# A two-block network kernel whose state-space scan handles channel groups one by one, and the same with groups taken in pairs

## The chip, the cores and the metric

One core of a Trainium2 chip runs the whole program. The metric is device time in microseconds (us). The kernel before has a median of 4561.05 us over 3 runs (4560.25 to 4565.51).

## What is computed

Two blocks run over 256 tokens of width 2048. Block one mixes windowed attention with a two-directional complex state-space scan (S5), followed by a product-key retrieval of experts (PEER); block two has a latent attention with a recurrent branch, and PEER again. All arithmetic is float32. The change touches only the scan. It is, for each of 64 groups of 16 channels, 64 complex states and two directions:

```
bu = einsum('bsgc,gnc->bsgn', u, b_bar)
_, states = lax.associative_scan(_ssm_combine, (a, bu), reverse=reverse, axis=1)
y = real(einsum('bsgn,gcn->bsgc', states, c_mat))
```

`_ssm_combine` multiplies the decays and adds the decayed left value. The results of both directions are added, `ssm_d * u` is added, and the sum goes through GELU to a gated linear unit.

## The kernel before

**Tiles and steps.** The 1024 scan channels are 8 tiles of 128 (index `k`, `SSM_K` = 8). A tile has 8 groups of 16 channels; two groups share the 128 partitions (2 x 64 states), which gives 4 pairs of groups (`q`, `PAIRS`) and two directions (`d`): 8 steps `s` a tile, with `q, d = s // 2, s % 2`. The complex recurrence is turned into two real scans: the product B times u is rotated by the phase of the step (multiplied by cosines and sines of the time index), two real scans run along time with a fixed decay, and the result is rotated back. C times the rotated states is then summed over the two directions into the output.

**What each engine does for a step.** GpSimd (POOL, L461) spreads the B matrices of the step into `b_pad`, 128 x 256, zero outside the step's 32 channels. TensorE (PE) transposes its two parts (`b_transposes`, L588), ScalarE (ACT) copies them to `b_t` (L956), and PE multiplies all 128 channels of u by them (`b_times_u`, L598) into the bank `mb[s % 2]`. ACT makes cosines and sines for the step (L961) from the phase that VectorE (DVE) worked out in the step before. DVE reads the bank (L1353, L1354; this counts up `bu_used`), forms the scan's inputs, scans (L1368), waits until the C product of the step before has read its states (`y_done`), rotates back (L1375, L1376) and forms `zr_e` (L1378, L1379; this counts up `de_ready`). PE multiplies by C (`c_times_states`, L610), 128 x 32 weights, into partitions 32q to 32q+31 of the bank `tb[1]`.

**Start and end of a tile.** PE transposes the tile's C matrices (L624), DVE masks and scales them (L1325 to L1344). After the eighth step DVE adds `ssm_d * u` (L1383). The tile's B and C matrices (`b_st`, `c_st`) are loaded by eight DMAs of ACT's queue (`load_bc`, L918 and L921). `reload_bc(k)` issues them for the next tile behind everything that ACT does in tile `k`, once the pads and C transposes of `k` are done.

**Dense work in between.** PE alone has other work in the scan: the projections that block one needs later. A *dense slot* (`dense_slot`, L531) is 8 matmuls of 128 x 512, each of which the profile shows as two passes, so 16. Eight slots fill the banks of group 0 (slots 0 to 3) and group 1 (slots 4 to 7). Tiles 0 to 5 have 8 slots each; tiles 6 and 7 have 4 each. ACT empties group 0 behind the sine of step 3 and group 1 behind the sine of step 7 (`dense_evac`, L947), in tiles 6 and 7 one group behind the sine of step 7.

**What sets the order.** Each engine's order is written out by hand, with semaphores between the engines. PE's order in a tile of 8 slots is: slot 0, C transposes, then the pads of steps 0 and 1 and the product of step 0, then for each step the B product of the next step, the transposes of the one after, one dense slot, and the C product of this step:

```
                for s in range(8):
                    if s < 7:
                        b_times_u(k, s + 1)
                    if s < 6:
                        b_transposes(k, s + 2)
                    if s + 1 in dense:
                        dense_slot(dense[s + 1], r, hT, r * 2)
                    c_times_states(k, s)
```

Weights of the dense slots come through a ring of 8 buffers of 1 MB, refilled by the SP queue.

Of the kernel before, what the change touches and what calls it, by code (L numbers as in the profile page):

```python
# [14 lines left out]
ds = bass.ds  # L15
# [73 lines left out]
def two_blocks(nc, a, out):  # L89

    ctx = ExitStack()
    with ctx:
# [26 lines left out]
        iota_t = cn[:, 128:384]  # L119
        mask_b = cn[:, 384:416].rearrange("p (q b) -> p q b", q=PAIRS)  # L120
        mask_c = cn[:, 416:544]
# [133 lines left out]
        (rA, rB, rZI, rZ, rD, rE, rF, rR, rBP, rBT, rCT, rCP, rPR) = cut(  # L255
            0, [512] * 8 + [512, 512, 512, 512, 256])
        two = lambda r: sc[:, r[0]:r[1]].rearrange("p (c n) -> p c n", c=2)
        bre_e, bim_e, z_in, z_out, zr_e, zi_e, phase, whole = map(two, (rA, rB, rZI, rZ, rD, rE, rF, rR))
        b_pad = sc[:, rBP[0]:rBP[1]].rearrange("p (i a b c) -> p i a b c", i=2, a=2, b=8)
        b_t = sc[:, rBT[0]:rBT[1]].rearrange("p (i a n) -> p i a n", i=2, a=2)  # L260
        c_t = sc[:, rCT[0]:rCT[1]].rearrange("p (d a n) -> p d a n", d=2, a=2)
# [168 lines left out]
        def _(pool):  # L430
# [10 lines left out]
            for half in range(2):  # L441
                rows = slice(64 * half, 64 * half + 64)
                for q in range(PAIRS):
                    st.link(pool.memset(mask_b[rows, q, 2 * q + half:2 * q + half + 1], 1.0))
                of_half = mask_c[rows, :].rearrange("p (q f c) -> p q f c", q=PAIRS, f=2)[:, :, half, :]
                st.link(pool.memset(of_half, 1.0))
# [7 lines left out]
            with pool.Fori(0, SSM_K) as k:  # L454

                pool.wait_ge(bc_loaded, k * BC + BC)
                for s in range(8):
                    q, d = s // 2, s % 2

                    pool.wait_ge(bt_done, k * 8 + s + 1)  # L460
                    pool.tensor_tensor(  # L461
                        b_pad[:, s % 2], b_st[:, :, d, q, :].unsqueeze(2).broadcast_to([P, 2, 8, 16]),
                        mask_b[:, q, :].unsqueeze(1).unsqueeze(3).broadcast_to([P, 2, 8, 16]),
                        ALU.mult).then_inc(bpad_ready, 1)

# [52 lines left out]
        def _(pe):  # L518
# [49 lines left out]

            pe.sem_inc(bt_done, 2)
            pe.sem_inc(bu_done, 2)  # L570
# [11 lines left out]

            def b_transposes(k, s):
                pe.wait_ge(bpad_ready, k * 8 + s + 1)

                pe.wait_ge(bt_evac, k * 8 + s + 2)
                for part in range(2):
                    tr = pe.transpose(tb[0][:, part * P:(part + 1) * P],  # L588
                                      b_pad[:, s % 2, part].rearrange("p b c -> p (b c)"), ident)
                tr.then_inc(bt_done, 1)  # L590

            def b_times_u(k, s):
                pe.wait_ge(bt_evac, k * 8 + s + 3)
                if s == 0:
                    pe.wait_ge(ct_evac, k + 1)
                pe.wait_ge(bu_used, k * 8 + s + 1)
                for part in range(2):
                    mm = pe.matmul(mb[s % 2][:, part * T:(part + 1) * T], b_t[:, s % 2, part, :],  # L598
                                   uT[:, ds(k, 1), :].rearrange("p a n -> p (a n)"), start=(part == 0), stop=True,
                                   skip_group_check=True)  # L600
                mm.then_inc(bu_done, 1)

            def c_times_states(k, s):
                q, d = s // 2, s % 2
                if s == 0:
                    pe.wait_ge(y_evac, k + 1)
                pe.wait_ge(de_ready, k * 8 + s + 3)

                for n, (j, rhs) in enumerate(((0, zr_e[:, 1, :]), (1, zr_e[:, 0, :]))):
                    mm = pe.matmul(tb[1][32 * q:32 * q + 32, 0:T], c_p[:, j, d, q, :], rhs,  # L610
                                   start=(d == 0 and n == 0), stop=(d == 1 and n == 1), skip_group_check=True)
                mm.then_inc(y_done, 1)

            def ssm_tile(k, r, slots):

                every = SLOTS // len(slots)
                dense = {n * every: b for n, b in enumerate(slots)}

                dense_slot(dense[0], r, hT, r * 2)
                pe.wait_ge(bc_loaded, k * BC + BC)  # L620

                pe.wait_ge(bu_used, k * 8 + 1)
# [4 lines left out]
                b_transposes(k, 0)  # L627
                b_times_u(k, 0)
                b_transposes(k, 1)
                for s in range(8):  # L630
                    if s < 7:
                        b_times_u(k, s + 1)
                    if s < 6:
                        b_transposes(k, s + 2)
                    if s + 1 in dense:
                        dense_slot(dense[s + 1], r, hT, r * 2)
                    c_times_states(k, s)


            pe.wait_ge(sp_done, 2)  # L640
            with pe.Fori(0, SSM_K - 2) as k:
                ssm_tile(k, k + R_QKV, range(SLOTS))
# [230 lines left out]
        def _(act):  # L873
# [23 lines left out]

            act.sem_inc(bt_evac, 2)
            norm_rms(0)
# [50 lines left out]
            def ssm_tile(k, i, groups):  # L950

                for s in range(8):

                    act.wait_ge(bt_done, k * 8 + s + 3)
                    act.wait_ge(bu_done, k * 8 + s + 1)
                    act.activation(b_t[:, s % 2].rearrange("p a n -> p (a n)"),  # L956
                                   tb[0][:, 0:2 * P], ACT.Copy).then_inc(bt_evac, 1)

# [6 lines left out]
            def reload_bc(k):  # L965

                act.wait_ge(bpad_ready, k * 8 + 8)
                act.wait_ge(ct_done, k + 1)
                load_bc(k + 1)
# [259 lines left out]
        def _(v):  # L1229
# [76 lines left out]
            def phase_1(k, s):  # L1306

                q, d = s // 2, s % 2
                return v.scalar_tensor_tensor(
# [9 lines left out]
            def ssm_tile(k):  # L1319
# [19 lines left out]

                v.wait_ge(y_done, k * 8 + 1)  # L1340
                st.wait()
# [3 lines left out]
                for s in range(8):  # L1345
                    q, d = s // 2, s % 2
                    both = lambda t: t.unsqueeze(1).broadcast_to([P, 2, T])
# [24 lines left out]

                    v.wait_ge(y_done, k * 8 + s + 1)
                    st.wait(z3)
# [5 lines left out]

                v.wait_ge(y_done, k * 8 + 9)
                kk = ds(k, 1)
# [457 lines left out]
```

## Time and profile before

| | us |
|---|---|
| median of 3 runs | 4561.05 |
| runs | 4560.25, 4561.05, 4565.51 |
| span of the profiled execution | 4559.0 |
| PE busy / DVE busy / ACT busy / POOL busy in it | 1629.2 / 3389.3 / 397.1 / 2108.9 |
| scan, from its first dense slot to the last tile's output | 83.2 to 692.2 |

The shares of the whole span say little of the scan: two long stretches of it are the expert retrievals, in which DVE and the gathers of POOL are busy and PE is not. The scan is one stretch of 609 us and is read by itself. A weight load (PEld) lies beside a running matmul. The own time of the profiled execution is not listed apart from its span; the span is 1.2 us under the lowest of the three runs.

### The profile page before, as it was taken

What the parts mean: (1) busy time and instruction counts of PE and PEld (TensorE: products, weight loads), DVE (VectorE), ACT (ScalarE), POOL (GpSimd) and SP (SyncE); (2) the same over time, 40 slices, a digit from 0 to 9 for tenths busy, and PEclk for the clock granted to TensorE, in tenths of its full rate; (3) what the DMA queues carried; (4) which work ended last, traced back from release to release, by engine and by line L of the source; (5) the groups of instructions that cost most, each with busy time, mean ns of one, the idle gap of its engine ahead of it and who ended that gap; (6) DMA issues with size and microseconds to landing.
All of it is one profiled execution on the core that took longest, in us unless ns stands there. A gap on an engine that the chain in (4) does not pass through costs nothing. (4 is left out here: it accounts for less than half of the span.)

```text
span 4559.0 us, 21846 instructions
## 1 busy us (share of the span) xinstructions
PE 1629.2 (36%) x5521; PEld 961.5 (21%) x5521; DVE 3389.3 (74%) x4309; ACT 397.1 (9%) x780; POOL 2108.9 (46%) x1162
## 2 busy tenths in 40 slices
PE   8999978998900000000000099888000000000000
PEld 6444434444800000000000066457000000000000
DVE  3777795301099999999999913411999999999999
ACT  1111114300100000000000013301000000000000
POOL 0000000000076777776777700000777767767767
PEclk9999989999955555555555599799555555555555
DMA  6343422344399999999999953132999999999999
GB/s 201 111 110 112 117 67 85 103 142 144 126 411 397 379 398 400 378 396 394 388 394 400 374 159 132 56 129 76 405 387 394 400 382 394 408 384 390 398 389 377
DMA packets 283029, 1286.59 MB, mean 282 GB/s; under 512 B 46993, under 2 KB 56033, under 8 KB 150881
## 3 DMA queue, kind: packets, MB, share of 16 engines
q0 software_dynamic: 147456, 1073.81, 57.7%
q1 hardware_dynamic: 100400, 200.81, 13.6%
q10 hardware_dynamic: 35120, 11.33, 1.0%
q8 instruction: 26, 0.43, 0.0%
q14 instruction: 27, 0.21, 0.0%
HBM read 1283.77 MB, written 2.10 MB: 282 GB/s over the span
## 5 line engine op out<-in xcount | busy, mean ns | idle before, releaser
L1578 DVE SCALAR_TENSOR_TENSOR xs<-big,sc,xs 128x2048 f32<-128x2048 f32 x512 | 1203.7, 2351 | 51.0 <-DVE sc L1568 2.1
L1560 DVE CUSTOM_DVE_ANT_0 big<-big,hs 128x2048 f32<-128x2048 f32 x512 | 1137.8, 2286 | 34.8 <-remote 10.3
L488 POOL DMA_INDIRECT big<-in_peer_down,sc x256 | 518.2, 2024 | 638.0 <-issue 635.4
L531 PE MATMUL bank<-wring,ht 128*128 128x512 f32 (+1 forms) x1792 | 778.5, 592 | 3.3 <-ACT ht L888 1.7
L488 POOL DMA_INDIRECT big<-in_peer_u,sc x256 | 518.2, 2024 | 405.0 <-DVE sc L1547 320.4
L488 POOL DMA_INDIRECT big<-in_peer_up,sc x256 | 506.0, 1977 | 247.6 <-DVE xs L1578 172.2
L488 POOL DMA_INDIRECT big<-in_peer_v,sc x256 | 506.1, 1977 | 246.6 <-DVE xs L1578 171.1
L772 PE MATMUL bank<-cn,sc 80*128 80x80 f32 x1 | 0.4, 393 | 1381.4 <-DMA sc<-in_rec_out_norm_g 1381.4
L531 PEld LDWEIGHTS bank<-wring,ht 128*128 128x128 f32 x1792 | 339.7, 192 | 402.1 <-issue 395.9
L545 PE MATMUL bank<-ht,wring 128*128 128x256 f32 x1792 | 387.9, 379 | 2.6 <-ACT ht L888 2.6
L545 PEld LDWEIGHTS bank<-ht,wring 128*128 128x128 f32 x1792 | 340.2, 190 | 49.6 <-issue 2.4
L461 POOL TENSOR_TENSOR sc<-big,cn 128x256 f32<-128x256 f32 x64 | 50.5, 795 | 605.4 <-DMA big<-in_ssm_c_im 319.4
L772 PEld LDWEIGHTS bank<-cn,sc 80*128 80x128 f32 x1 | 0.2, 180 | 1381.6 <-DMA sc<-in_rec_out_norm_g 1381.6
L1073 ACT ACTIVATE sc<-sc 128x16 f32<-128x16 f32 x32 | 6.9, 215 | 2436.0 <-DVE sc L1560 2436.0
L1512 DVE COPY sc<-ht 128x256 f32 (+1 forms) x32 | 9.2, 287 | 242.5 <-ACT ht L1062 242.5
L657 PE MATMUL bank<-wring,hs 128*128 128x512 f32 x256 | 117.9, 601 | 5.2 <-ACT hs L984 5.2
L507 POOL MEMSET big<- 128x384 f32 x1 | 0.4, 418 | 235.4 <-DVE big L1750 235.4
L1375 DVE TENSOR_TENSOR sc<-sc,big 128x512 f32<-128x512 f32 x64 | 43.9, 687 | 77.7 <-PE bank L610 77.5
L1499 DVE TENSOR_TENSOR xs<-bank,xs 128x512 f32 x8 | 5.2, 685 | 113.1 <-PE bank L531 113.1
L610 PE MATMUL bank<-sc 128*32 128x256 f32 x256 | 72.6, 409 | 46.3 <-DVE sc L1379 46.3
L1368 DVE TENSOR_TENSOR_SCAN sc<-sc 128x256 f32<-128x256 f32 x128 | 84.1, 697 | 1.3 <-DVE sc L1314 0.2
L1481 DVE TENSOR_TENSOR big<-bank,big 128x512 f32 x8 | 5.2, 685 | 101.0 <-PE bank L531 101.0
(308 smaller groups left out, 2055.2 us busy)
## 6 DMA issues: line engine op xcount, KB each, us to landing
wring<-in_w_in SPq DMA_DIRECT2D x84, 1024.0 KB, 5.3
wring<-in_w_out SPq DMA_DIRECT2D x32, 1024.0 KB, 5.0
wring<-in_w_attn_o SPq DMA_DIRECT2D x16, 1024.0 KB, 5.1
wring<-in_peer_w_query SPq DMA_DIRECT2D x16, 1024.0 KB, 5.0
wring<-in_peer_w_q SPq DMA_DIRECT2D x16, 1024.0 KB, 5.0
wring<-in_glu_w_a SPq DMA_DIRECT2D x8, 1024.0 KB, 5.0
wring<-in_glu_w_b SPq DMA_DIRECT2D x8, 1024.0 KB, 5.0
big<-in_peer_down,sc POOLq DMA_INDIRECT x256, 9.5
```

The costliest lines, as they stand in the source:

```text
L461: pool.tensor_tensor(b_pad[:, s % 2], b_st[:, :, d, q, :].unsqueeze(2).broadcast_to([P, 2, 8, 16]), mask_b[:, q, :].unsqueeze(1).unsqueeze ...
L488: pool.indirect_dma_start(out=gslot[:, slot, :], out_offset=None, in_=table[0], in_offset=bass.IndirectOffsetOnAxis(ap=usub(rST)[:, b * TO ...
L531: mm = pe.matmul(dense_bank[2 * pair + t][:, 0:w_cols], lhs[:, k, t * P:(t + 1) * P], wslot[:, b, kk * w_cols:(kk + 1) * w_cols], start=(k ...
L545: mm = pe.matmul(dense_bank[2 * g + c // 2][:, (c % 2) * T:(c % 2 + 1) * T], wslot[:, b, kk * 512 + c * P:kk * 512 + (c + 1) * P], rhs[:, ...
L610: mm = pe.matmul(tb[1][32 * q:32 * q + 32, 0:T], c_p[:, j, d, q, :], rhs, start=(d == 0 and n == 0), stop=(d == 1 and n == 1), skip_group_ ...
L657: mm = pe.matmul(dense_bank[2 * pair + t][:, :], yT[:, k, t * P:(t + 1) * P], wslot[:, b, kk * 512:(kk + 1) * 512], start=(k == 0), stop=( ...
L1073: act.activation(sub(rGE)[:, b * TOPK:(b + 1) * TOPK], sub(rAC)[:, b * TOPK:(b + 1) * TOPK], ACT.Gelu).then_inc(gelu_ready, 1)
L1368: z3 = st.add(v.tensor_tensor_scan(zo, radius, zi, 0.0, ALU.mult, ALU.add))
L1375: st.add(v.tensor_tensor(zr_e, both(z_out[:, 0, :]), e, ALU.mult))
L1512: st.link(v.tensor_copy(w1, kscore[:, ds((unit - base) * 256, 256)]))
L1560: v.tensor_tensor_reduce(gslot[:, slot, :], gslot[:, slot, :], h[:, t, :], 1.0, 0.0, ALU.mult, ALU.add, sub(rAC)[:, b * TOPK + kk:b * TOPK ...
L1578: v.scalar_tensor_tensor(x[:, t, :], gslot[:, slot, :], wt[:, kk:kk + 1], x[:, t, :], ALU.mult, ALU.add).then_inc(gused[slot], 1)
```

## The change

Steps are taken in pairs `m` = 0 to 3, steps 2m and 2m+1: `q_and_d` gives both the same direction and neighbouring pairs of groups (q = 0, 1, then 0, 1 backwards, then 2, 3, and 2, 3 backwards).

- `b_pad` holds the whole tile: POOL makes it in four operations of half the size, PE turns it in four transposes into one bank, ACT copies it with one copy of 128 x 512.
- `b_times_u(k, m)` multiplies only the 32 channels of a step (rows 32q to 32q+31 of the array); the two steps of a pair alternate, one bank each. `c_times_states(k, m)` alternates the pair's two column strips.
- There are two buffers for the rotated states; `y_done` counts pairs, and a step waits only for the pair before its own.
- PE's order is new. The C and B transposes come first, then slot 0, then the B product of pair 0. In pair m of a tile with 8 slots come two dense slots with the B product of pair m+1 ahead of the second, then the C product. Pair 0 has only slot 1 left, with the B product of pair 1 ahead of it. The loop over tiles 0 to 5 is written out.

```
+            def b_times_u(k, m):
+
+                pe.wait_ge(bu_used, k * 8 + 2 * m + 2)
                 for part in range(2):
+                    for s in (2 * m, 2 * m + 1):
+                        q, d = q_and_d(s)
+                        rows = slice(32 * q, 32 * q + 32)
+                        mm = pe.matmul(mb[s % 2][:, part * T:(part + 1) * T], b_t[rows, d, part, :],
+                                       uT[rows, k, :], start=(part == 0),
+                                       stop=True, skip_group_check=True)
+                        if part == 1:
+                            mm.then_inc(bu_done, 1)
+
+            def c_times_states(k, m):
+                if m == 0:
                     pe.wait_ge(y_evac, k + 1)
+                pe.wait_ge(de_ready, k * 8 + 2 * m + 4)
+
+                for n in range(2):
+                    for s in (2 * m, 2 * m + 1):
+                        q, d = q_and_d(s)
+                        mm = pe.matmul(tb[1][32 * q:32 * q + 32, 0:T], c_p[:, n, d, q, :], states[s % 2][:, 1 - n, :],
+                                       start=(d == 0 and n == 0), stop=(d == 1 and n == 1), skip_group_check=True)
                 mm.then_inc(y_done, 1)
 
             def ssm_tile(k, r, slots):
 
-                every = SLOTS // len(slots)
-                dense = {n * every: b for n, b in enumerate(slots)}
-
-                dense_slot(dense[0], r, hT, r * 2)
+                per = len(slots) // 4
                 pe.wait_ge(bc_loaded, k * BC + BC)
...
+                pe.wait_ge(bpad_ready, k * 4 + 4)
+                pe.wait_ge(bt_evac, k + 1)
+                for d in range(2):
+                    for part in range(2):
+                        j = d * 2 + part
+                        tr = pe.transpose(tb[0][:, j * P:(j + 1) * P],
+                                          b_pad[:, d, part].rearrange("p q f c -> p (q f c)"), ident)
+                tr.then_inc(bt_done, 1)
+                dense_slot(slots[0], r, hT, r * 2)
+                pe.wait_ge(bt_evac, k + 2)
+                pe.wait_ge(ct_evac, k + 1)
                 b_times_u(k, 0)
...
+                for m in range(4):
+                    for b in slots[max(1, m * per):m * per + per]:
+                        if b == slots[m * per + per - 1] and m < 3:
+                            b_times_u(k, m + 1)
+                        dense_slot(b, r, hT, r * 2)
+                    if m < 3 and not slots[max(1, m * per):m * per + per]:
+                        b_times_u(k, m + 1)
+                    c_times_states(k, m)
...
             def ssm_tile(k, i, groups):
 
+                act.wait_ge(bt_done, k + 2)
+                act.wait_ge(bu_done, k * 8 + 2)
+                act.activation(b_t.rearrange("p d a n -> p (d a n)"), tb[0][:, :], ACT.Copy).then_inc(bt_evac, 1)
                 for s in range(8):
...
-                    v.wait_ge(y_done, k * 8 + s + 1)
+                    v.wait_ge(y_done, k * 4 + s // 2 + 1)
```

ACT's order for the rest of a tile is as before: sines 0 to 3, the emptying of group 0, sines 4 to 7, the emptying of group 1, the eight load DMAs.

**First place: PE at the start of a tile of 8 slots.** The names are those of the banks and buffers; `L531` is a dense slot, `L624` and `L588` are the C and B transposes, `L598` a B product, `L610` a C product. Before:

```order
L531 MATMUL bank<-wring,ht 128x512 [waits wfull0]
L531 MATMUL bank<-wring,ht 128x512 x7
...
L622 ISA [waits bc_loaded]
L624 MATMUL bank<-cn,big 128x128 [waits bu_used]
L624 MATMUL bank<-cn,big 128x128 x3
...
L588 MATMUL bank<-cn,sc 128x128 [waits bt_evacuated]
...
L598 MATMUL bank<-hs,sc 128x256 x2
...
L598 MATMUL bank<-hs,sc 128x256 [waits bu_used,bt_evacuated]
...
L531 MATMUL bank<-wring,ht 128x512 [waits wfull1]
...
L610 MATMUL bank<-sc 32x256 [waits states_ready,y_evacuated]
```

Now (`L615` C transposes, `L623` B transposes, `L590` B product, `L604` C product):

```order
L615 MATMUL bank<-cn,big 128x128 [waits bu_used,bc_loaded]
L615 MATMUL bank<-cn,big 128x128 x3
L623 MATMUL bank<-cn,sc 128x128 [waits bt_evacuated,bpad_ready]
L623 MATMUL bank<-cn,sc 128x128 x3
L531 MATMUL bank<-wring,ht 128x512 [waits wfull0,pair_evac0]
L531 MATMUL bank<-wring,ht 128x512 x7
L590 MATMUL bank<-hs,sc 128x256 [waits bu_used,ct_evacuated,bt_evacuated]
L590 MATMUL bank<-hs,sc 128x256 x3
L590 MATMUL bank<-hs,sc 128x256 [waits bu_used]
L590 MATMUL bank<-hs,sc 128x256 x3
L531 MATMUL bank<-wring,ht 128x512 [waits wfull1]
...
L604 MATMUL bank<-sc 32x256 [waits states_ready,y_evacuated]
```

The wait for the loaded matrices now stands ahead of slot 0, and two B products stand in a row with no slot between them.

**Second place: PE from slot 2 to slot 4, in the changed kernel.** Slot 3 is the last of group 0:

```order
L531 MATMUL bank<-wring,ht 128x512 [waits wfull2]
...
L590 MATMUL bank<-hs,sc 128x256 [waits bu_used]
...
L531 MATMUL bank<-wring,ht 128x512 [waits wfull3]
...
L604 MATMUL bank<-sc 32x256 [waits states_ready]
...
L531 MATMUL bank<-wring,ht 128x512 [waits wfull4,pair_evac1]
```

Slot 3 was in step 2, ahead of the C product of step 2; it is now in pair 1, behind the B product of steps 4 and 5.

**Third place: ACT in the middle of a tile, in the changed kernel** (`L959` is a sine, `L947` the emptying of a dense bank, `wused3` the end of slot 3, `wused7` of slot 7):

```order
L959 ACTIVATE big<-sc 128x512 [waits states_ready,phase_ready]
L947 ISA [waits wused3]
L947 ACTIVATE big<-bank 128x512
L947 ISA
L947 ACTIVATE big<-bank 128x512
L957 REGISTER_ALU
L959 ACTIVATE big<-sc 128x512 [waits states_ready,phase_ready]
```

The sine of step 4 stands behind the emptying that waits for slot 3, as before; what moved is slot 3 on PE.

## Rows read from the trace of the kernel before

**Rows 1.** Busy time by stretch: start:end, length, engines, granted clock, DMA share, GB/s.
```profile
170.00:248.00 78.00, 73.88 (x213) 34.55 (x212) 58.23 (x112) 9.73 (x20) 5.97 (x8) 1.00 0.40 113
248.00:562.00 314.00, 297.39 (x849) 138.70 (x848) 232.95 (x448) 38.91 (x80) 24.70 (x32) 0.99 0.39 112
562.00:631.00 69.00, 51.40 (x148) 24.90 (x147) 59.15 (x112) 8.42 (x18) 6.78 (x8) 0.88 0.21 67
```
**Rows 2.** Who waited for whom, scan only: us in total, times, longest us.
```profile
DVE sc L1375 <- PE bank L610: 77.5, 33, 3.4
```
**Rows 3.** Timeline, one step on PE: start us, us, engine, line, operation, count.
```profile
190.78 1.05 PE L610 MATMUL bank<-sc 128*32 128x256 f32 x4
191.76 1.13 PE L598 MATMUL bank<-hs,sc 128*128 x4
192.72 0.38 PE L588 MATMUL bank<-cn,sc 128*128 128x128 f32 x2
192.94 7.03 PE L531 MATMUL bank<-wring,ht 128*128 128x512 f32 x16
199.90 1.05 PE L610 MATMUL bank<-sc 128*32 128x256 f32 x4
```
**Rows 4.** Timeline, one step on DVE, and the start of the next.
```profile
94.52 0.69 DVE L1353 TENSOR_TENSOR sc<-bank,big 128x512 f32<-128x512 f32 x1 [0.19 <-DVE sc L1344]
95.12 0.68 DVE L1354 TENSOR_TENSOR sc<-bank,big 128x512 f32<-128x512 f32 x1
99.15 0.68 DVE L1375 TENSOR_TENSOR sc<-sc,big 128x512 f32<-128x512 f32 x1
...
101.15 0.68 DVE L1353 TENSOR_TENSOR sc<-bank,big 128x512 f32<-128x512 f32 x1
```
**Rows 5.** Timeline, end of tile 1 and start of tile 2, PE.
```profile
236.94 1.05 PE L610 MATMUL bank<-sc 128*32 128x256 f32 x4
...
241.15 7.13 PE L531 MATMUL bank<-wring,ht 128*128 128x512 f32 x16
248.12 0.60 PE L624 MATMUL bank<-cn,big 128*128 128x128 f32 x4
```
**Rows 6.** The same place, ACT's queue: the first of the loads.
```profile
237.49 0.38 ACTq L918 DMA_DIRECT2D big<-in_ssm_b_re  x1
```
**Rows 7.** The same place and an earlier one, POOL: the pads.
```profile
170.97 0.62 POOL L461 TENSOR_TENSOR sc<-big,cn 128x256 f32<-128x256 f32 x1 [3.69 <-PE bank L588]
...
246.29 1.20 POOL L461 TENSOR_TENSOR sc<-big,cn 128x256 f32<-128x256 f32 x2 [42.62 <-DMA big<-in_ssm_c_im]
```
**Rows 8.** Busy time by stretch around an idle time of PE (columns as in 1).
```profile
567.00:573.00 6.00, 0.00 (x0) 0.00 (x0) 5.97 (x14) 0.90 (x2) 0.35 (x1) 0.82 0.00 0
573.20:575.00 1.80, 1.80 (x4) 0.50 (x4) 1.80 (x4) 0.00 (x0) 0.00 (x0) 0.50 0.00 0
575.00:576.80 1.80, 1.80 (x5) 1.41 (x5) 1.80 (x5) 0.00 (x0) 0.00 (x0) 0.50 0.00 0
577.30:584.30 7.00, 7.00 (x18) 3.01 (x16) 6.97 (x14) 0.90 (x2) 1.77 (x1) 0.98 0.00 0
```
**Rows 9.** Timeline, ACT behind step 3: bank emptied, sine of step 4, DVE of step 3.
```profile
200.21 1.08 ACT L947 ACTIVATE big<-bank 128x512 f32 x2 [6.74 <-PE bank L531]
200.99 0.69 DVE L1375 TENSOR_TENSOR sc<-sc,big 128x512 f32<-128x512 f32 x1 [1.26 <-PE bank L610]
...
201.44 0.64 ACT L961 ACTIVATE big<-sc 128x512 f32<-128x512 f32 x1
```
**Rows 10.** Timeline, the scan's first PE work; DVE's first bank read in tiles 6 and 7, last operation of step 7.
```profile
83.16 7.13 PE L531 MATMUL bank<-wring,ht 128*128 128x512 f32 x16 [0.80 <-DVE sc L1296]
...
566.34 0.69 DVE L1353 TENSOR_TENSOR sc<-bank,big 128x512 f32<-128x512 f32 x1 [0.20 <-DVE sc L1344]
...
635.82 0.69 DVE L1353 TENSOR_TENSOR sc<-bank,big 128x512 f32<-128x512 f32 x1 [0.20 <-DVE sc L1344]
...
689.03 0.42 DVE L1379 TENSOR_TENSOR sc<-sc 128x256 f32<-128x256 f32 x1
```

More of the change, by code:

```diff
@@ L253, in cut @@
             return res
-        (rA, rB, rZI, rZ, rD, rE, rF, rR, rBP, rBT, rCT, rCP, rPR) = cut(
-            0, [512] * 8 + [512, 512, 512, 512, 256])
+        (rA, rB, rZI, rZ, rD, rD2, rE, rF, rR, rBP, rBT, rCT, rCP, rPR) = cut(
+            0, [512] * 9 + [512, 512, 512, 512, 256])
         two = lambda r: sc[:, r[0]:r[1]].rearrange("p (c n) -> p c n", c=2)
-        bre_e, bim_e, z_in, z_out, zr_e, zi_e, phase, whole = map(two, (rA, rB, rZI, rZ, rD, rE, rF, rR))
-        b_pad = sc[:, rBP[0]:rBP[1]].rearrange("p (i a b c) -> p i a b c", i=2, a=2, b=8)
-        b_t = sc[:, rBT[0]:rBT[1]].rearrange("p (i a n) -> p i a n", i=2, a=2)
+        bre_e, bim_e, z_in, z_out, zi_e, phase, whole = map(two, (rA, rB, rZI, rZ, rE, rF, rR))
+        states = (two(rD), two(rD2))
+        b_pad = sc[:, rBP[0]:rBP[1]].rearrange("p (d a q f c) -> p d a q f c", d=2, a=2, q=PAIRS, f=2)
+        b_t = sc[:, rBT[0]:rBT[1]].rearrange("p (d a n) -> p d a n", d=2, a=2)
+        q_and_d = lambda s: (s // 4 * 2 + s % 2, s // 2 % 2)
         c_t = sc[:, rCT[0]:rCT[1]].rearrange("p (d a n) -> p d a n", d=2, a=2)
@@ L442, in _ @@
                 rows = slice(64 * half, 64 * half + 64)
-                for q in range(PAIRS):
-                    st.link(pool.memset(mask_b[rows, q, 2 * q + half:2 * q + half + 1], 1.0))
+                st.link(pool.memset(mask_b[rows, half:half + 1], 1.0))
                 of_half = mask_c[rows, :].rearrange("p (q f c) -> p q f c", q=PAIRS, f=2)[:, :, half, :]
@@ L456, in _ @@
                 pool.wait_ge(bc_loaded, k * BC + BC)
[L457 to L464, printed above, removed]
+                pool.wait_ge(bt_done, k + 1)
+                for d in range(2):
+                    for part in range(2):
+                        pool.tensor_tensor(
+                            b_pad[:, d, part], b_st[:, part, d].unsqueeze(2).broadcast_to([P, PAIRS, 2, 16]),
+                            mask_b.unsqueeze(1).unsqueeze(3).broadcast_to([P, PAIRS, 2, 16]),
+                            ALU.mult).then_inc(bpad_ready, 1)
             pool.wait_ge(y_evac, SSM_K + 1)
@@ L592, in b_times_u @@
[L592 to L601, printed above, removed]
@@ L603, in c_times_states @@
-            def c_times_states(k, s):
-                q, d = s // 2, s % 2
-                if s == 0:
-                    pe.wait_ge(y_evac, k + 1)
[L607 to L611, printed above, removed]
+                    for s in (2 * m, 2 * m + 1):
[6 more added lines that the diff above has]
+                            mm.then_inc(bu_done, 1)
@@ L626, in ssm_tile @@
                 tr.then_inc(ct_done, 1)
-                b_transposes(k, 0)
-                b_times_u(k, 0)
[L629 to L637, printed above, removed]
+                pe.wait_ge(bpad_ready, k * 4 + 4)
+                pe.wait_ge(bt_evac, k + 1)
+                for d in range(2):
+                    for part in range(2):
+                        j = d * 2 + part
[5 more added lines that the diff above has]
+                pe.wait_ge(ct_evac, k + 1)
+                b_times_u(k, 0)
+                for m in range(4):
[6 more added lines that the diff above has]
+                    c_times_states(k, m)
             pe.wait_ge(sp_done, 2)
-            with pe.Fori(0, SSM_K - 2) as k:
+            for k in range(SSM_K - 2):
                 ssm_tile(k, k + R_QKV, range(SLOTS))
@@ L1345, in ssm_tile @@
                 for s in range(8):
-                    q, d = s // 2, s % 2
+                    q, d = q_and_d(s)
+                    zr_e = states[s % 2]
                     both = lambda t: t.unsqueeze(1).broadcast_to([P, 2, T])
```

26 lines of the change are left out of this document (8 added, 18 removed).

## The prediction, made before the changed kernel had run

> **What bounds the kernel now.** The page gives shares over 4559 us, but the change touches one stretch of 609 us, so I first cut the trace there by busy time. In tiles 1 to 5 PE is busy 371 of 392 us and DVE 291 [rows 1]: PE bounds the tiles with eight dense slots. In tile 6, with four slots, DVE is busy 59 of 69 us and PE 51: there DVE's chain of steps bounds. The list of waits agrees: DVE stood 77.5 us before L1375 until PE had made a C product that was queued behind a dense slot [rows 2]. The timeline then gives the prices. A PE step is 9.12 us from C product to C product: 0.98 for the C product, 0.96 for the B product, 0.22 for two transposes, 6.96 for the slot [rows 3]. A DVE step that does not wait is 6.6 us (94.52 to 101.15); it has read the bank 1.3 us after its start, and reaches the state buffer at 4.6 [rows 4]. A tile with eight slots takes on average (566.34 - 94.52) / 6 = 78.6 us from first bank read to first bank read [rows 4, 10].
>
> **What it removes.** Per tile, 12 of 16 transposes: 12 x 0.11 = 1.3 us of PE. The B and C products go from 16 of 0.96 to 0.98 us to 8 pairs. No row shows two strips of the array together, so a pair is bounded: 0.98 if two strips cost as one, 1.84 if they run one behind the other (8 passes of 0.215 and one change-over of 0.12, from [rows 3]). I take 1.3, just under the middle: each strip's two passes must follow each other, but the other strip's can lie beside the second. That frees 8 x 1.94 - 8 x 1.3 = 5.1 us, together some 6.5 us of PE a tile. The Trainium skill, "TensorE: Matmul & The Clock Gate", Part 3 (Packing small matmuls), says that matmuls on different strips start about 4 ns apart and a pack takes the time of one matmul; no row here shows it, and by it the pair would be 0.98 and the whole change 53 us slower instead of 68. The waits of DVE at L1375 shrink too. POOL's pads halve in size and in number. DVE has the same instructions as before. This is work; what counts is the order.
>
> **What it moves, first place: the load is uncovered.** Slot 7 ends at 236.94. ACT then issues eight loads, the first at 237.49, and POOL can start at 246.29: 9.35 us [rows 5 to 7]; the other tile boundaries of the trace are up to 0.7 shorter, and I take 9.0. Before, the C product of step 7 and slot 0 of the next tile lay in it, and PE met the loaded matrices only at 248.12. Now the C and B transposes wait for the load ahead of slot 0, and slot 7 lies ahead of the last C product. So PE has one C product (1.3) to do in 9.0 us, then waits for the pads: four operations of half the size of one that took 0.62, so 0.3 to 0.6 each, 1.8 in all. Queued behind it on PE is everything, slot 0 included.
>
> **Second place: pair 0 has no cover.** The B product of pair 1 needs both banks read, which is one DVE step and 1.3 us after DVE's start: 6.6 + 1.3 = 7.9. No slot lies between it and the B product of pair 0.
>
> **Third place: slot 3 holds back a sine.** ACT makes the sine of step 4 only after emptying group 0. From slot 3's end (199.9) to the end of that sine (202.1) it is 2.1 us [rows 3, 9]. Slot 3 now comes after the B product of pair 2, when DVE has already finished step 3; DVE waits for it.
>
> **The clock.** After 6 us without matmuls the granted clock is 0.50, the 1.2 GHz level, for the next two products, 3.6 us of work, and 0.98, the 2.4 GHz level, after that [rows 8]: a loss of 1.8 us. Both new idle times are longer, so I charge 1.8 twice a tile, bounds 0 and 3.6 each (none lost, or twice as long).
>
> **The walk through a tile of eight slots**, from the moment the load has landed, with 6.9 for a slot (its 6.96 less a change-over that is in the products):
> - transposes with their wait for the pads 2.4; slot 0 6.9; clock 1.8: 11.1. B product of pair 0 to DVE's first read 1.4 (four passes of C to L1375 take 1.1 [rows 3, 9], and 0.3 for the pair): DVE starts at **12.5**.
> - plus 7.9: 20.4. B product 1.3, slot 1 6.9, clock 1.8, C product 1.3: 31.7. DVE has finished step 1 at 25.7, so PE is the later.
> - slot 2 6.9, B product 1.3, slot 3 6.9: 46.8. Sine 2.1: DVE starts step 4 at 48.9 (it had been free since about 41).
> - plus 7.9: 56.8; PE had slot 4 done by 55. B product 1.3, slot 5 6.9, C product 1.3, slots 6 and 7 13.8: **80.1**. Load 9.0: **89.1**.
>
> That is 10.5 more than 78.6, the sum of 16 to 17 us of new idle time of PE and of lost clock, less the work freed. DVE reads the first bank of tile 0 at 83.2 [rows 10] + 0.9 + 6.9 + 1.4 = 92.4 instead of 94.5, as the matrices of tile 0 are there long before. So tile 6 starts at 92.4 + 6 x 89.1 = 627.0 instead of 566.3 [rows 10]: **+60.7**.
>
> **Tiles 6 and 7, four slots.** The B product of pair 1 goes at 7.9 after DVE's start, of pair 2 at 13.3 + 7.9 = 21.2; then slot 1, clock and C product end at 32.5. DVE waits 1.2 there for the buffer, and about as long a pair later. The B product of pair 3 goes at 35.7; with slot 2, clock, C product and slot 3 it is 53.9. Load 9.0 and start 12.5: 75.4, against 69.5 before (635.82 - 566.34 [rows 10]): **+5.9**. In tile 7 DVE needs 8 x 6.63 + 2.4 = 55.4 for its eight steps, before 689.45 - 635.82 = 53.6 [rows 10]: **+1.8**. The written-out PE loop costs nothing that a row could show: tiles 6 and 7 were written out before, and a slot there takes 7.0 us too [rows 8]. DVE, ACT and the weight ring have slack where PE idles.
>
> **The sum**: 60.7 + 5.9 + 1.8 = 68.4 us. All that follows the scan waits for its output, so the end moves by as much. The profiled span of 4559.0 becomes 4627.4; it stands 2.05 under the median, which becomes 4561.05 + 68.4 = 4629.5, rounded **4630**.
>
> **Rivals.**
> - *Two strips cost as one* (a pair 0.98). Six pairs lie on the walk: 6 x 0.32, 0.3 less of slow clock, 2.2 a tile, 13 us, and 2 in the last tiles: 4615. For it: the strips are separate parts of the array, and a pair's outputs lie in separate banks or partitions. Against: each product is two passes that reuse one strip. The page named above makes this rule.
> - *Strips run one behind the other*, so that this part of the change does nothing (a pair 1.84): 6 x 0.54 and 0.5 of clock, 3.7 a tile, 22 us, and 3: 4655.
> - *The clock does not fall, or work between the idle times restores it*: less 1.8 x 2 x 6 and 5 in the last tiles, 27 us: 4603. Against it are rows 8.
> - *The load is covered, and the tiles get shorter: faster.* If the new matrices were there when the last C product ends, and slot 3 were done in time for the sine, the walk would be 0.9 + 6.9 + 1.4 + 7.9 + 9.5 + 16.4 + 16.4 + 15.1 = 74.5: 4.1 a tile under 78.6, 25 us, and some 5 in the last: about 4531. That is what 6.5 us less of PE work promises. It decides in favour if the load lands within 1.3 us of slot 7's end instead of 9.0, and ACT's order speaks against it: the loads are still last.
>
> **Chances.** Forecast 0.48; strips as one 0.18; strips one behind the other 0.18; clock 0.07; load covered 0.05; the rest 0.04, longer idle times and more slow clock than charged. A measurement of this kernel tells 0.2%, 9 us, from no change. All but the covered load are over that: slower 0.93, same 0.02, faster 0.05. The range runs from the clock case to strips in sequence with a load of 9.4 and some clock more: 4602 to 4665.
>
> **What would show it.** Right: tiles of 89 us from first bank read to first bank read; PE idle 7 to 8 us behind the last C product of a tile, released by the load; 8 us between the first two B products, released by DVE's L1354; DVE idle 7 to 8 us before step 4, released by ACT's sine; granted clock 0.5 at the start of slots 0 and 1; a pair at 1.2 to 1.4 us. Wrong: transposes right behind the last C product, tiles under 78 us, or a DVE that never waits at step 4.

## The result, and the profile after

The changed kernel takes **4629.49 us** (median of 4 runs, 4626.96 to 4632.71), beside 4561.3 for the kernel before (4 runs, 4560.25 to 4565.51). The ratio is 1.0148, with a 95% interval of 1.0134 to 1.0163: slower by 68.2 us, where 68.4 were forecast. The profiled execution has a span of 4628.2 us and a mean granted clock of 0.670 (before 4559.0 and 0.683). All four engines are busy for less time than before, PE for 26 us less (1603.1), and the kernel takes longer.

Busy time by stretch of the changed kernel; the columns are those of [rows 1], the five busy times those of PE, PEld, DVE, ACT and POOL. The stretches are tile 0, tile 1, tiles 2 to 5 and tile 6:

```profile
83.00:170.00 87.00, 69.01 (x201) 30.37 (x202) 59.16 (x116) 8.38 (x15) 0.02 (x1) 0.92 0.38 114
170.00:259.00 89.00, 71.10 (x201) 31.30 (x201) 56.96 (x112) 7.58 (x13) 1.45 (x4) 0.88 0.33 99
259.00:613.00 354.00, 284.08 (x800) 125.40 (x800) 227.85 (x448) 30.33 (x52) 5.88 (x16) 0.89 0.33 100
613.00:688.00 75.00, 47.03 (x136) 20.88 (x136) 56.96 (x112) 6.61 (x11) 1.47 (x4) 0.75 0.21 62
```

A tile of eight slots has 71 of 89 us of PE in it, before 74 of 78 [rows 1]. PE no longer bounds these tiles, nor does DVE with 57 of 89: 18 us of each tile are PE standing still, before 4. The granted clock, 1.00 before, is 0.88.

To measure a tile I take DVE's first scan in it (L1367, and L1368 of the kernel before). The differences from tile to tile are 89.6, 89.0, 88.6, 88.8, 88.7, 88.6 and, from tile 6 to tile 7, 75.0. Before they were 79.9, 78.1, 79.7, 78.1, 78.0, 78.0 and 69.5.

The list of waits in the scan (us in total, times, longest us):

```profile
PE bank L590 <- DVE sc L1353: 93.8, 18, 8.1
PE bank L615 <- DMA big<-in_ssm_c_im: 49.9, 7, 7.7
DVE sc L1352 <- PE bank L590: 60.0, 8, 8.3
DVE sc L1352 <- ACT big L959: 49.6, 6, 8.3
...
DVE sc L1374 <- PE bank L604: 19.4, 10, 2.6
```

The first four are new. The first is for the most part the B product of pair 1 with no cover (the uncovered pair): eight of its 18 waits are 8.1 us long. The second is the load that nothing covers. The third is DVE waiting for the first B product of a tile, which now stands behind slot 0: 8.11 us in tile 1, while slot 0 runs from 172.42 to 181.02. This wait hangs on the load too; with the load out of the way (e1) it falls from 60.0 to 21.6 us in total. The fourth is the sine behind slot 3. DVE's waits for C products, 77.5 us before [rows 2], are the last row, 19.4: the change does what it says there.

The timeline of PE over tile 1 (start us, us, engine, line, operation, count, and in brackets the idle time ahead and what ended it), to hold against [rows 3, 5]:

```profile
161.17 1.06 PE L604 MATMUL bank<-sc 128*32 128x256 f32 x8
169.88 1.11 PE L615 MATMUL bank<-cn,big 128*128 128x128 f32 x4 [7.65 <-DMA big<-in_ssm_c_im]
171.51 1.12 PE L623 MATMUL bank<-cn,sc 128*128 128x128 f32 x4 [0.52 <-POOL sc L461]
172.42 8.68 PE L531 MATMUL bank<-wring,ht 128*128 128x512 f32 x16
181.02 1.13 PE L590 MATMUL bank<-hs,sc 32*128 32x256 f32 x8
190.26 2.08 PE L590 MATMUL bank<-hs,sc 32*128 32x256 f32 x8 [8.10 <-DVE sc L1353]
192.26 9.07 PE L531 MATMUL bank<-wring,ht 128*128 128x512 f32 x16
201.26 1.06 PE L604 MATMUL bank<-sc 128*32 128x256 f32 x8
202.25 7.13 PE L531 MATMUL bank<-wring,ht 128*128 128x512 f32 x16
209.31 1.13 PE L590 MATMUL bank<-hs,sc 32*128 32x256 f32 x8
210.38 7.13 PE L531 MATMUL bank<-wring,ht 128*128 128x512 f32 x16
217.44 1.06 PE L604 MATMUL bank<-sc 128*32 128x256 f32 x8
...
227.33 1.13 PE L590 MATMUL bank<-hs,sc 32*128 32x256 f32 x8 [1.77 <-DVE sc L1353]
...
250.38 1.06 PE L604 MATMUL bank<-sc 128*32 128x256 f32 x8
258.95 1.12 PE L615 MATMUL bank<-cn,big 128*128 128x128 f32 x4 [7.52 <-DMA big<-in_ssm_c_im]
```

Three idle times, as the walk had them: behind the last C product of a tile, before the B product of pair 1, and a short one before the B product of pair 3. A pair of B products takes 210.38 - 209.31 = 1.07 us and a pair of C products 202.25 - 201.26 = 0.99: a pair on two strips costs what one product cost before (0.98 for C), or 0.11 us more (0.96 for B [rows 3]). Slot 0 takes 8.60 us (172.42 to 181.02) and slot 1 takes 9.00 (192.26 to 201.26); all others of the tile take 6.97 to 7.06.

The granted clock behind the second idle time; the first stretch is the B product of pair 1, the others lie in slot 1 (columns as above):

```profile
189.90:192.10 2.20, 1.84 (x8) 1.18 (x8) 2.20 (x6) 0.00 (x0) 0.00 (x0) 0.50 0.00 0
192.30:194.30 2.00, 2.00 (x5) 0.97 (x4) 2.00 (x5) 0.63 (x1) 0.00 (x0) 0.50 0.00 0
194.30:196.30 2.00, 2.00 (x4) 0.84 (x3) 1.97 (x5) 0.00 (x0) 0.00 (x0) 0.53 0.00 0
196.30:198.30 2.00, 2.00 (x6) 0.89 (x5) 2.00 (x5) 0.00 (x0) 0.00 (x0) 1.00 0.00 0
```

PE is at 0.50, the 1.2 GHz level, from 190.3 to about 196.3. That is 6 us of work after 8 us of nothing, not the 3.6 us that the kernel before showed [rows 8].

The middle of the tile, ACT and DVE (rows between them left out):

```profile
217.65 1.08 ACT L947 ACTIVATE big<-bank 128x512 f32 x2 [16.73 <-PE bank L531]
...
218.62 0.63 ACT L959 ACTIVATE big<-sc 128x512 f32<-128x512 f32 x1
...
219.36 0.69 DVE L1352 TENSOR_TENSOR sc<-bank,big 128x512 f32<-128x512 f32 x1 [8.27 <-ACT big L959]
```

ACT waits for slot 3, which ends at 217.44, empties group 0, and only then makes the sine of step 4. DVE has been idle for 8.27 us. From slot 3's end to DVE's read it is 1.92 us (forecast 2.1).

Most of the load's time is its issue. Of the 8.7 us from the end of slot 7 (161.17) to the first transposes (169.88), ACT's queue spends 6.2 on issuing the eight DMAs, the first at 161.82 and the last done at 167.98; one of them alone shows 2.02 us. From there to the transposes it is 1.9 us.

### The profile page after: what moved, and what is told of

It is laid out like the page before. It is cut to its first block and busy times, and to the rows that moved or that the text cites. A ratio compares the mean times of both kernels' runs of the same rounds, so it can differ in the third digit from the quotient of the medians.

```text
span 4628.2 us, 21289 instructions
## 1 busy us (share of the span) xinstructions
PE 1603.1 (35%) x5425; PEld 936.2 (20%) x5425; DVE 3378.1 (73%) x4309; ACT 381.1 (8%) x724; POOL 2071.0 (45%) x1124
## 5 line engine op out<-in xcount | busy, mean ns | idle before, releaser
L531 PE MATMUL bank<-wring,ht 128*128 128x512 f32 (+1 forms) x1792 | 805.9, 609 | 2.4 <-ACT ht L888 1.7
L531 PEld LDWEIGHTS bank<-wring,ht 128*128 128x128 f32 x1792 | 349.6, 198 | 433.4 <-issue 427.6
L461 POOL TENSOR_TENSOR sc<-big,cn 128x128 f32<-128x128 f32 x32 | 11.9, 402 | 674.7 <-DMA big<-in_ssm_c_im 674.7
L1352 DVE TENSOR_TENSOR sc<-bank,big 128x512 f32<-128x512 f32 x64 | 43.9, 686 | 109.7 <-PE bank L590 60.0
L1367 DVE TENSOR_TENSOR_SCAN sc<-sc 128x256 f32<-128x256 f32 x128 | 81.3, 678 | 1.1
L590 PE MATMUL bank<-hs,sc 32*128 32x256 f32 x256 | 45.7, 484 | 93.8 <-DVE sc L1353 93.8
```

The source lines that it names most:

```text
L461: pool.tensor_tensor(b_pad[:, d, part], b_st[:, part, d].unsqueeze(2).broadcast_to([P, PAIRS, 2, 16]), mask_b.unsqueeze(1).unsqueeze(3).br ...
L531: mm = pe.matmul(dense_bank[2 * pair + t][:, 0:w_cols], lhs[:, k, t * P:(t + 1) * P], wslot[:, b, kk * w_cols:(kk + 1) * w_cols], start=(k ...
L590: mm = pe.matmul(mb[s % 2][:, part * T:(part + 1) * T], b_t[rows, d, part, :], uT[rows, k, :], start=(part == 0), stop=True, skip_group_ch ...
L1352: st.add(v.tensor_tensor(bre_e, both(mb[s % 2][:, 0:T]), e, ALU.mult))
L1367: z3 = st.add(v.tensor_tensor_scan(zo, radius, zi, 0.0, ALU.mult, ALU.add))
```

## The experiments

Eight kernels. The first four ask where the 68 us come from and whether the parts add up; e5 and e6 ask what the strips of the array are worth; e7 and e8 test the clock and the load by themselves. The first four share one set of runs of the kernel before (median 4561.56), the others a second (4562.64), so that a comparison across the two sets carries 1.1 us.

### e1: the load early

```
 # ACT, ssm_tile
+                    if s == 1 and reload:
+                        reload_bc(k)
 ...
-                reload_bc(k)
```

> The changed kernel with one edit: ACT issues the eight loads of the next tile's matrices behind the sine of step 1 instead of behind the emptying of group 1; they only need the pads and C transposes of the tile, which are done at its start. Theory (the uncovered load costs its whole wait): PE's 7.5 us of idle time, 0.5 us for the pads and about 2.5 us of slow clock vanish at six tile ends and some 8 us at the seventh: 71 us less than the changed kernel, about 4558. Rival (DVE's work at the tile's end bounds there, the load only hides it): less than 15 us are gained and the wait before the C transposes goes to DVE.

**4555.95 us**, ratio 0.9988 (0.9978 to 0.9998), 73.5 under the changed kernel, where 71 were expected. Tiles of 77.5 to 78.5 us, 66.1 from tile 6 to tile 7. The timeline of PE in e1 at the same tile boundary:

```profile
159.09 1.06 PE L604 MATMUL bank<-sc 128*32 128x256 f32 x8
160.08 0.66 PE L615 MATMUL bank<-cn,big 128*128 128x128 f32 x4
...
161.01 7.03 PE L531 MATMUL bank<-wring,ht 128*128 128x512 f32 x16
167.97 1.13 PE L590 MATMUL bank<-hs,sc 32*128 32x256 f32 x8
177.20 2.08 PE L590 MATMUL bank<-hs,sc 32*128 32x256 f32 x8 [8.09 <-DVE sc L1353]
```

The transposes stand right behind the last C product, take half as long, and slot 0 takes 6.96 (161.01 to 167.97) instead of 8.60. Moving eight DMA issues gives back more than the whole loss; the other two idle times stay. From the start of the last C product to the B product of pair 0 it is 8.9 us (159.09 to 167.97) instead of 19.85 (161.17 to 181.02). Of these 11.0, 8.2 are idle time of PE (7.65 for the load and 0.52 for the pads), 1.6 the slow clock in slot 0 and about 1 the slow clock in the eight transposes. Where the load is issued is thus the largest part of the damage.

### e2: the sine of step 4 before group 0 is emptied

```
-                ssm_tile(k, k, {3: 0, 7: 1})
+                ssm_tile(k, k, {5: 0, 7: 1})
```

> The changed kernel with one edit: ACT empties group 0 behind the sine of step 5 instead of step 3. Theory (PE bounds the middle of the tile, DVE's idle time there costs only what PE then waits for at the B product of pair 3): DVE's 8.3 us of idle time before step 4 vanish, PE's 1.8 us before the third B product too, 6 x 1.8 = 11 us less than the changed kernel, about 4618. Rival (DVE's idle time counts in full): about 48 us less, 4581.

**4609.62 us**, ratio 1.0106 (1.0089 to 1.0123): 19.9 less than the changed kernel. Tiles of 86.9, 86.5, 85.5, 85.3, 85.5 and 85.4. That is 2.4 to 3.5 a tile, not 1.8 as forecast and not the 8 of the rival: DVE's 8.27 us of idle time were nearly all hidden behind PE. The 1.77 us before the B product of pair 3 are gone. The remainder, 0.6 to 1.7 us a tile, is in most tiles a slightly shorter idle time at the load (6.91 to 7.54 us, in the changed kernel 7.08 to 7.65) and, in tiles 2 to 5, less slow clock: in tile 4 the rows of slots 0 and 1 show 7.81 and 8.64 us, in the changed kernel 8.59 and 9.03. Slots 0 and 1 of tile 1 show none of this (9.05 and 9.27). Why the slow stretches are shorter there, no row tells.

### e3: a slot between the first two B products

```
-                dense_slot(slots[0], r, hT, r * 2)
                 pe.wait_ge(bt_evac, k + 2)
                 pe.wait_ge(ct_evac, k + 1)
                 b_times_u(k, 0)
+                dense_slot(slots[0], r, hT, r * 2)
 ...
+                    if m == 0:
+                        b_times_u(k, 1)
                     c_times_states(k, m)
```

The B product of pair 0 goes ahead of slot 0, and that of pair 1 behind slot 1.

> The changed kernel with one edit in PE's order: the B product of pair 0 stands ahead of slot 0, and slots 0 and 1 stand between it and the B product of pair 1. Theory (8.1 us of PE idle time and 3 us of slow clock between the first two B products are the cost): D7 moves from 80 to 70 us of a tile, 10.5 x 6, and DVE starts 7 us earlier in tiles 6 and 7: 77 us less than the changed kernel, about 4552. Rival (what pair 0 waits for now is found elsewhere, at the load): under 30 us less.

**4570.95 us**, ratio 1.0022 (1.0012 to 1.0031): 58.5 less, where 77 were expected (D7 in the expectation is the end of slot 7, 80.1 in the walk). The idle time of 8.1 us is gone, but a tile takes 80.0 to 82.1 us instead of the 78.6 that this makes. PE in e3, from the end of tile 0 to the start of tile 1:

```profile
131.51 1.13 PE L590 MATMUL bank<-hs,sc 32*128 32x256 f32 x8 [1.76 <-DVE sc L1353]
...
142.32 14.00 PE L531 MATMUL bank<-wring,ht 128*128 128x512 f32 x32
...
168.17 2.08 PE L590 MATMUL bank<-hs,sc 32*128 32x256 f32 x8 [0.77 <-ACT sc L954]
170.17 16.09 PE L531 MATMUL bank<-wring,ht 128*128 128x512 f32 x32
186.20 1.13 PE L590 MATMUL bank<-hs,sc 32*128 32x256 f32 x8
```

and busy time and clock behind the first of these rows:

```profile
132.60:134.60 2.00, 2.00 (x6) 0.94 (x5) 2.00 (x5) 0.00 (x0) 0.00 (x0) 0.71 0.88 335
134.60:136.60 2.00, 2.00 (x4) 0.87 (x3) 1.97 (x5) 0.63 (x1) 0.00 (x0) 0.50 0.00 1
```

Behind the load, which e3 leaves uncovered, PE is as slow as before: slots 0 and 1 take 16.03 us (170.17 to 186.20) where two slots take 13.93 at the upper level (142.32 to 156.25), and the B product of pair 0 takes 2.00. PE also waits 0.77 us ahead of it for ACT's copy of the transposed B matrices, which slot 0 used to cover. And a second slow stretch now comes behind an idle time of 1.76 us (tile 0, slot from 132.57 on, and so in five of the six tiles, not in tile 4), which before the same product of the changed kernel (1.77 us) had cost nothing. The expectation had taken the slow clock away with the idle time; part of it only moved.

### e4: all three at once

ACT as in e1, group 0 emptied behind the sine of step 4 (`{4: 0, 7: 1}`), and on PE, from slot 0 on:

```
+                if per == 2:
+                    plan = "S B0 S B1 S C0 S B2 S C1 S B3 S C2 S C3"
+                else:
+                    plan = "B0 S B1 S C0 B2 S C1 B3 S C2 C3"
```

where `S` is the next dense slot and a number is a pair. The eighth slot lies between C2 and C3, so that every product of a tile of eight slots has a slot ahead of it.

> All three waits taken away: loads behind the sine of step 1, group 0 emptied behind the sine of step 4, and PE's order in a tile of eight slots S B0 S B1 S C0 S B2 S C1 S B3 S C2 S C3 (S a slot, B and C the products of the numbered pair), in tiles 6 and 7 B0 S B1 S C0 B2 S C1 B3 S C2 C3. Theory (pairing frees 7 us of PE a tile, and only the order hid it): a tile takes 67 to 69 us against 88.8 in the changed kernel and 78.6 before, 140 us less than the changed kernel, about 4490, and 70 less than before. Rival (pairing itself costs time, by strips or by the clock): no better than before, 4561.

**4490.82 us** (4487.5 to 4495.65), ratio 0.9847 (0.9831 to 0.9864). This beats both kernels, and the expected time is met. Busy time by stretch of e4, tile 0 and then tiles 1 to 5:

```profile
83.00:150.00 67.00, 65.24 (x199) 28.29 (x197) 56.73 (x111) 7.69 (x13) 1.92 (x4) 1.00 0.43 134
150.00:485.00 335.00, 326.94 (x994) 143.22 (x992) 284.84 (x558) 37.39 (x63) 9.78 (x20) 1.00 0.43 131
```

Tiles 0 to 4 take 67.4 us, tile 5 takes 65.1. PE is busy 327 of 335 us, the clock is 1.00, and a tile has two idle times of PE left: 1.03 us before the B product of pair 1 and 0.73 before the last C product. The three repairs alone gave 73.5, 19.9 and 58.5, in sum 152; together they gave 138.7. They overlap: the 1 us a tile that e2 saves at the load and in slow slots can't be saved again where e1 has covered the load. The plan is not exactly their union either: its order of slots and products is a different one from e3's.

### e5: the strips not alternated

```
-                for part in range(2):
-                    for s in (2 * m, 2 * m + 1):
+                for s in (2 * m, 2 * m + 1):
+                    for part in range(2):
```

and the same in the C product: all passes of one step, then all of the other, on e4.

> The kernel of e4_all_three, with the two steps of a pair no longer alternating: both products of one strip, then both of the other. Theory (passes start in order and a pass waits for its own strip, so strips overlap only where neighbours differ): a pair takes about 1.6 us instead of 1.0, eight pairs a tile in six tiles, about 30 us more than e4_all_three, near 4520. Rival (the engine looks ahead and starts a later pass on a free strip): no change, 4491.

**4490.19 us**, ratio 0.9843 (0.9827 to 0.986): no change from e4. The first 0.2 us of one pair of B products, of these instructions alone (length, busy time of PE and of PEld, clock, DMA share, GB/s; x counts the passes that run in the stretch); e4:

```profile
115.83:116.03 0.20, 0.20 (x2) 0.20 (x4) 1.00 0.00 0
```

and e5:

```profile
115.86:116.06 0.20, 0.20 (x2) 0.20 (x4) 1.00 0.00 0
```

Two passes run at once in either. Written as all of step 2m and then all of step 2m+1, they still start in twos, 13 ns apart instead of 7. The alternating loop of the change is not needed; which part of the chip or of the compilation lets the second step's passes start beside the first's, no row tells.

### e6: both steps of a pair on one strip

```
-                        q, d = q_and_d(s)
+                        q, d = q_and_d(2 * m)
```

in both products, on e4.

> The kernel of e4_all_three, with both steps of a pair sent to the strip of its first step (rows in the B product, output partitions in the C product); the second step's B and C products are therefore computed from the first one's channels and added into its output. Theory (two strips cost as one, and that is what pairing gains): a pair takes 1.85 us instead of 1.0, 0.86 x 8 x 6 = 41 us more than e4_all_three, near 4532. Rival (the pair is short for another reason, such as 32 rows or columns being faster in themselves): a pair stays near 1.0 and the time at 4491.

**4552.16 us** (4545.28 to 4557.26), ratio 0.9977 (0.9967 to 0.9987), 61.3 over e4. PE in e6 at the start of tile 0:

```profile
91.17 1.99 PE L590 MATMUL bank<-hs,sc 32*128 32x256 f32 x8
93.09 7.13 PE L531 MATMUL bank<-wring,ht 128*128 128x512 f32 x16
100.83 1.99 PE L590 MATMUL bank<-hs,sc 32*128 32x256 f32 x8 [0.61 <-DVE sc L1360]
102.75 8.83 PE L531 MATMUL bank<-wring,ht 128*128 128x512 f32 x16
111.51 1.91 PE L604 MATMUL bank<-sc 128*32 128x256 f32 x8
```

and the first 0.2 us of the second of these products, as for e5:

```profile
100.83:101.03 0.20, 0.20 (x1) 0.20 (x2) 1.00 0.65 147
```

One pass at a time, and a pair takes 1.92 us (91.17 to 93.09) or 1.84 (C, 111.51 to 113.35). The upper bound of the prediction was 1.84; the two strips give 0.85 us a pair, 6.9 a tile, of which 0.4 comes back as shorter idle time (0.61 us instead of 1.03). Tile 2, of 73.9 us, is 6.5 longer than in e4. Tiles 0, 1, 3 and 4, of 75.5, have a slow clock on top: slot 2 takes 8.76 us (102.75 to 111.51) after an idle time of only 0.61. The expected 41 us left that out, and tiles 6 and 7: from tile 6 to tile 7 it is 75.9 us instead of 65.5, and tile 7 is 8.3 longer from its first scan to its last. A pair of B products there, behind idle times of 3.1 and 3.4 us, takes 3.2 to 3.7 us (537.40 to 541.08, 583.93 to 587.17).

### e7: idle time filled with work that nobody needs

```
                 b_times_u(k, 0)
+                if per == 2:
+                    for n in range(8):
+                        pe.matmul(tb[0][:, :], ident, hT[:, 2 * n:2 * n + 2, :].rearrange("p k n -> p (k n)"),
+                                  start=True, stop=True)
```

The changed kernel with a slot's worth of matmuls in the uncovered pair.

> The changed kernel with 8 extra matmuls of 128 x 512 (16 passes, 6.9 us) behind the B product of pair 0 in tiles 0 to 5, into the bank that held the transposed B matrices, where PE otherwise idles 8.1 us. Nothing reads them. Theory (the idle time costs a second time, by the clock: the B product of pair 1 and slot 1 take 11.1 us instead of 8.1): granted clock 1.0 there, 3.0 us less a tile, 18 us less than the changed kernel, about 4611. Rival (those two are slow for another reason, such as reads that collide with DVE's): no change, 4629.

**4612.19 us**, ratio 1.011 (1.0093 to 1.0127): 17.3 less than the changed kernel, with more work. PE of e7 around that place:

```profile
186.10 1.13 PE L590 MATMUL bank<-hs,sc 32*128 32x256 f32 x8 [1.03 <-DVE sc L1357]
187.16 7.13 PE L531 MATMUL bank<-wring,ht 128*128 128x512 f32 x16
```

The granted clock is 1.00 in every stretch from 181 to 199. So the clock's share of the uncovered pair is 17.3 us over six tiles, 2.9 a tile: 0.94 in the B product (2.00 instead of 1.06) and 1.94 in slot 1 (9.00 instead of 7.06). The waiting itself, 8.1 us a tile, is the larger share and is untouched. The tiles do not show this evenly: five of the six are 3.1 to 3.9 us shorter than in the changed kernel, and tile 2 only 0.8, because its slot 5 runs slow behind an idle time of 1.77 us (307.00 to 315.76, 8.76 us).

### e8: slot 0 behind the transposes, in the kernel before

```
-                dense_slot(dense[0], r, hT, r * 2)
                 pe.wait_ge(bc_loaded, k * BC + BC)
 ...
                 b_transposes(k, 0)
+                dense_slot(dense[0], r, hT, r * 2)
                 b_times_u(k, 0)
```

> The kernel before with one edit: slot 0 moved behind the C transposes and the first B transposes, so that the load is uncovered and nothing is paired. Theory (the order ahead of slot 0, not the pairing, exposes the load): PE idles about 5 us at each of six tile ends, plus 0.6 for the pads and 1.8 of slow clock, less small waits that vanish, 6 to 7 us a tile, 38 us more than before, about 4600. Rival (the load is late only because the changed kernel ends its tiles sooner): under 10 us more, 4570.

**4594.77 us**, ratio 1.0075 (1.0059 to 1.0092): 32 slower than the kernel before. PE of e8 at the start of tile 1:

```profile
164.34 1.11 PE L623 MATMUL bank<-cn,big 128*128 128x128 f32 x4 [4.09 <-DMA big<-in_ssm_c_im]
165.25 0.63 PE L588 MATMUL bank<-cn,sc 128*128 128x128 f32 x2
165.68 8.95 PE L531 MATMUL bank<-wring,ht 128*128 128x512 f32 x16
```

This one move, with nothing of pairs or strips, makes the load's idle time and the slow clock behind it (slot 0 takes 8.79 us) and lengthens tiles to 83.1 to 85.0 us. The idle time is 4.1 to 4.9 us instead of 7.6, because in the old order slot 7 ends two C products before the tile does, and PE waits 2.2 us between them for DVE while the load is under way. The six tiles cost 33 us; ahead of them and in tile 6 the edit saves some (DVE's first bank read comes 3.4 us earlier, and from tile 6 to tile 7 it is 65.9 us instead of 69.5), which the expected 38 had left out.

## Why the prediction was right, and where it was not

**The walk.** The forecast was 89.1 us a tile and 75.4 from tile 6 to tile 7; the chip took 88.6 to 89.6, and 75.0. The same points in tile 1, from the start of its transposes (169.88):

| | forecast | measured |
|---|---|---|
| DVE's first read | 12.5 | 12.4 (182.28) |
| B product of pair 1 | 20.4 | 20.4 (190.26) |
| C product of pair 0 done | 31.7 | 32.4 (202.25) |
| DVE starts step 4 | 48.9 | 49.5 (219.36) |
| B product of pair 3 | 56.8 | 57.5 (227.33) |
| slot 7 done | 80.1 | 80.5 (250.38) |
| transposes of the next tile | 89.1 | 89.1 (258.95) |

All three new idle times are where the walk had them, released by what it named: the load, DVE's second bank read, ACT's sine. The step on which everything hung, "the load is uncovered", was tested from both sides: e1 takes it back and gains 73.5 us, e8 puts it into the kernel before and loses 32. The second, "pair 0 has no cover", holds as well: its idle time is the 8.1 us of the waits, and e3 and e7 get 58.5 and 17.3 us back there. The third, "slot 3 holds back a sine", has its 8.27 us of idle DVE, but e2 shows that little of it reached the end: 19.9 us over the tiles, of about 50.

**Two terms were mis-sized and cancelled.** "I take 1.3, just under the middle" for a pair of strips: it is 1.07 for B and 0.99 for C. The rival *two strips cost as one* was the truth of that term, and the reason against it, that each product is two passes that reuse one strip, does not hold: the other strip's passes lie wholly beside them. That made the walk about 1.5 us a tile too long. The Trainium skill, "TensorE: Matmul & The Clock Gate", Part 3 (Packing small matmuls), has the pack at the time of one matmul and its tiles starting about 4 ns apart; the trace agrees on the time (0.99 against 0.98 us for C, 1.07 against 0.96 for B) and shows starts 7 ns apart.

The other is "I charge 1.8 twice a tile" for the clock. The row behind that charge [rows 8] showed 3.6 us of slow work; behind the uncovered pair it is 6 us, and e7 prices it at 2.9, while slot 0 behind the load lost 1.6. That is 4.5 instead of 3.6, inside the bounds of 0 and 3.6 each. And "6.9 for a slot" was too little by 0.16 where a product follows (202.25 to 209.31 is 7.06), 0.9 in a tile. So 1.5 too much stood against 1.8 too little, and the load (8.6 for 9.0) and the sine (1.92 for 2.1) took up the rest. Tile 6 has the same: the B product of pair 3 comes 36.9 us after DVE's first read (forecast 35.7), and the load ends 7.6 us after slot 3 (forecast 9.0).

There is luck in the total as well. In the profiled executions the scan's last output comes at 757.89 instead of 691.71 (the start of L1382, and of L1383 before): the change moved it by 66.2 us, not by 68.4. The spans differ by 69.2; the other 3.0 us lie behind the scan, where nothing was changed. That part takes 3867.3 us in the profile before and 3869.5 to 3874.0 in the nine others, so it differs between executions by some us. That the median came within 0.5 us of the forecast is luck of that size; the order of the work, read from the trace, carried the sign and nearly all of the amount.

**The ends.** DVE's first read came at 92.6 (forecast 92.4), and tile 7 takes 49.8 us from its first scan to its last, before 47.9: 1.9 more, forecast 1.8. Up to the scan's output only 1.1 of it is left (56.95 us from the first read, before 55.89), because the last C product took 1.92 us at the slow clock before and takes 1.06 now.

**The rival on the other side**, that a covered load and an early sine make tiles shorter than before, said 74.5 us a tile and 4531. As a statement on the change it was wrong: the loads are still last. As a price it was too modest: e4, which adds a slot between the first B products, has tiles of 67.4 us and a time of 4490.82. With pairs at 1.03 the change frees 1.3 + 8 x (1.94 - 1.03) = 8.6 us of PE a tile instead of the 6.5 that I counted, and PE's time without work falls from 20.7 us in tiles 1 to 5 [rows 1] to 8.1 (335.0 - 326.9), 2.5 a tile. Together that is 11.1, and 78.6 - 67.4 = 11.2.

**What stays open.** When the clock falls. Idle times of 8 us bring it down every time, those of 1.8 us in no tile of the changed kernel, in five of six of e3 and in one of six of e7, and 0.61 us does so in four of the six tiles of e6. No run separates the cases, and I give no rule. Also not tried was an early load in the kernel before: its pads of steps 6 and 7 read the loaded buffer until late in the tile, so an early load needs a second buffer there. In the changed kernel all pads are made at the tile's start, and this is what makes e1 possible without one.

## What to carry to other kernels

When a change frees work on the bounding engine, walk one period of the new order before counting the freed work: here 8.6 us a tile were freed, but PE's idle time rose from 4 to 18 us, nearly all of it three waits whose position had moved against a load, against a one-step chain of DVE and against a bank that ACT empties. Every wait at the head of an in-order queue needs work ahead of it that lasts as long as the wait, and the first to repair is the one that a mere earlier issue removes (eight DMA issues, 73 us). On PE a long idle time can cost more than its length, here 8.1 us of waiting and 2.9 of slow clock behind it; even dead matmuls in that gap made the kernel faster.

## What the runs showed of the chip that was not expected

- Two 32-row or 32-column strips of the array run float32 products fully side by side, though each product is several passes: 1.07 and 0.99 us for eight passes, 1.92 and 1.84 on one strip (e4 and e6). Passes on two strips start 7 ns apart when alternated, 13 ns apart when not (e5), and the time is the same.
- The slow stretch after an idle time is not one length: 3.6 us of work in the kernel before [rows 8], about 6 us behind the uncovered pair of the changed one.
- A slot can run slow after 0.6 us of idle time (8.76 instead of 7.06 us, e6), while 1.77 us cost nothing in the changed kernel's order (tiles 0 to 5).
- Eight small DMA issues in a row are a long wait by themselves: 6.2 us on ACT's queue (161.82 to 167.98, changed kernel), before the last of them lands.
